# Gate and up projections by seven block products per tile pair, feed-forward in two chunks

## What is computed

```python
def half_ffn(x, g, w_gate, w_up, w_down):
    h = rmsnorm(x, g)
    return 0.5 * ((jax.nn.silu(h @ w_gate) * (h @ w_up)) @ w_down)
```

## Time and profile before

| what | value |
|---|---|
| median of three runs | 2231.39 us (2229.24 to 2231.44) |
| profiled execution | 2230.26 us |
| its span | 2228.7 us |
| PE, DVE, ACT, POOL busy | 98%, 48%, 35%, 3% |
| matmuls recorded | 18340 |
| weights and data read, written | 188.5 MB, 8.05 MB |
| mean rate of the transfers | 89 GB/s |

### The profile page before, as it was taken

One profiled execution on the slowest core, in us unless ns is written; L12 is line 12 of the kernel. 1 busy time (PEld: TensorE's weight loads), 2 busy tenths in 40 slices (PEclk: granted clock), 3 DMA queues, 4 the chain that ended last, 5 costly groups with the idle time before them and its releaser, 6 DMA issues.

```text
span 2228.7 us, 41911 instructions
## 1 busy us (share of the span) xinstructions
PE 2174.9 (98%) x18340; PEld 2115.3 (95%) x18340; DVE 1067.8 (48%) x1536; ACT 769.9 (35%) x1060; POOL 66.8 (3%) x140
## 2 busy tenths in 40 slices
PE   7999999999988999999999999999999999999998
PEld 7999999998887899999999999999997599999997
DVE  5444433586555544444334444433568545444332
ACT  5222222344244442222223222222357633222222
POOL 0000000100110000000000000000102300000000
PEclk9999999999998999999999999999999999999999
DMA  4333333433200323333333333333324323333231
GB/s 135 99 87 94 93 90 86 115 89 82 77 7 2 100 87 94 94 87 93 95 88 95 89 92 96 91 88 98 100 67 143 125 76 104 87 95 95 88 92 59
DMA packets 355286, 199.15 MB, mean 89 GB/s; under 512 B 10070, under 2 KB 350194, under 8 KB 355096
## 3 DMA queue, kind: packets, MB, share of 16 engines
q1 hardware_dynamic: 346768, 174.49, 27.3%
q0 software_dynamic: 6160, 19.84, 3.1%
q10 hardware_dynamic: 2176, 2.15, 0.3%
HBM read 188.52 MB, written 8.05 MB: 88 GB/s over the span
## 4 chain that ended last, share of the span: by engine, by line
PE 93%; DVE 4%; ACT 2%; issue 1%; DMA 0%; ACTq 0%; DVEq 0%
PE PS L2136 84%; PE PS L2244 4%; PE PS L2784 1%; PE PS L2703 1%; PE PS L2717 0%; PE PS L2686 0%; DVE X L1681 0%; PE PS L2151 0%; PE PS L2769 0%; PE PS L2706 0%; PE PS L2589 0%; PE PS L2312 0%; DVE wlo L1356 0%; DMA prow_f<-in_ln_ffn 0%; DVE skX L1960 0%
## 5 line engine op out<-in xcount | busy, mean ns | idle before, releaser
L2136 PE MATMUL PS<-hh,whi 128*128 128x260 f32 x3600 | 729.4, 284 | 3.1 <-DVE hl L2059 1.8
L2136 PE MATMUL PS<-hh,wlo 128*128 128x260 f32 x3600 | 726.0, 283 | 0.0
L2136 PE MATMUL PS<-hl,whi 128*128 128x260 f32 x3600 | 725.0, 283 | 0.0
L1356 DVE TENSOR_TENSOR wlo<-stage,whi 128x1024 fp32r<-128x1024 f32 x337 | 412.3, 1223 | 471.2 <-ACT whi L771 467.6
L2136 PEld LDWEIGHTS PS<-hh,whi 128*128 128x128 f32 x3600 | 556.4, 189 | 6.0 <-DVE small L1495 1.5
L2136 PEld LDWEIGHTS PS<-hh,wlo 128*128 128x128 f32 x3600 | 555.6, 189 | 0.0
L2136 PEld LDWEIGHTS PS<-hl,whi 128*128 128x128 f32 x3600 | 554.2, 188 | 0.0
L771 ACT ACTIVATE whi<-stage 128x1024 fp32r<-128x1024 f32 x337 | 352.9, 1049 | 282.4 <-PE PS L2136 270.6
L2136 PE MATMUL PS<-act_h,whi 128*128 128x260 f32 x1408 | 284.0, 283 | 0.0
L2136 PE MATMUL PS<-act_h,wlo 128*128 128x260 f32 x1408 | 283.2, 282 | 0.0
L2136 PE MATMUL PS<-act_l,whi 128*128 128x260 f32 x1408 | 282.5, 282 | 0.0
(11 more groups left out here) (427 smaller groups left out, 1554.1 us busy)
## 6 DMA issues: line engine op xcount, KB each, us to landing
stage<-in_ffn_w_gate SPq DMA_DIRECT2D x88, 512.0 KB, 3.8
stage<-in_ffn_w_up SPq DMA_DIRECT2D x88, 512.0 KB, 3.8
stage<-in_ffn_w_down SPq DMA_DIRECT2D x64, 512.0 KB, 3.7
stage<-in_w_in_e SPq DMA_DIRECT2D x28, 512.0 KB, 3.8
stage<-in_ffn_w_down SPq DMA_DIRECT2D x32, 384.0 KB, 3.4
stage<-in_w_in_o SPq DMA_DIRECT2D x20, 512.0 KB, 3.7
stage<-in_w_out_e SPq DMA_DIRECT2D x8, 512.0 KB, 3.7
stage<-in_w_out_o SPq DMA_DIRECT2D x8, 512.0 KB, 3.7
```

The source lines that it names most:

```text
L1356: dve.tensor_tensor(wlo[:, slot, :], stage[:, s % STAGE_SLOTS, :], whi[:, slot, :].bitcast(F32), ALU.subtract).then_inc(lo_ready, 1)
L2136: mm = pe.matmul(psum[:, half, :], w, x(k)[:, half * HALF:(half + 1) * HALF], start=first and w is hi and x is rhs_hi, stop=last and w is lo)
```

## The change

For the output tile pairs 2 to 10 of each feed-forward (MODES "S"), gate and up are each computed as one **group** of seven block products; pairs 0 and 1 (HEAD, "P") stay plain units. A group takes the two output tiles as block columns of the weights, even and odd contraction tiles as block rows, and the two token halves as block columns of the input, which makes a 2x2 by 2x2 block product; the scheme has seven products and sums around them. A product (`block_product`) is 4 contraction tiles x 3 = 12 matmuls of 260 columns into one PSUM bank, so a group has 84 matmuls where two units have 96.

- The weights of a group (1 MB) come in one transfer to half of a doubled staging place (`stage`, `stage_x`). ACT and DVE split them in four batches: a (1024 columns), b (512, into `w4h` and `w4l`), c and d (1024 each). Between these DVE forms four sums of 4x128 columns in place (`sum_of`), which batches c and d then split. The batches of the next group are made while this one's products run.
- The sums of the input blocks are formed once per feed-forward during the head: four operations of 260 columns per tile of `ht_h` and `ht_l`, a copy of `xb` by ACT, and a split of 1040 columns.
- Products go to four PSUM banks, in the order P1, P6, P2, P5, P3, P7, P4, and each bank is used again. ACT copies P1 to `snapT`; DVE adds the others in seven block sums (`add`): U2, C11, V, C12, U3, C22, C21. Then gate is multiplied by rstd, Silu is applied by ACT, and up multiplies it without rstd, which the down projection's update applies.
- The feed-forward goes in two CHUNKS: pairs 0 to 5, then the down projection of their 12 tiles, then pairs 6 to 10 and the down projection of 10 tiles; activations have 12 places instead of 22. A down output tile has two pieces per chunk (8 and 4, 6 and 4 contraction tiles), and its update is two DVE operations (`update_down`) in each chunk.
- The stage loops are written out, and a plan (`BATCHES`, `LOADS`) sets slots, places and counts of the waits ahead of time.

```diff
+CHUNKS = ((0, 6), (6, 11))
+MODES = ("PP", "PP") + ("SS",) * 9
+HEAD = 2
+DOWN_PAIRS = (2, 3, 1, 0, 2, 1, 0, 3)
+DOWN_ORDER = [(0, 0), (1, 0), (0, 1), (1, 1)] + [(m, p) for m in range(2, 8) for p in range(2)]
+ORDER = ("P1", "P6", "P2", "P5", "P3", "P7", "P4")
+PRODUCTS = {"P1": ("a", 0), "P2": ("a", 1), "P3": ("d", 1), "P4": ("b", 0), "P5": ("c", 0), "P6": ("c", 1), "P7": ("d", 0)}
...
+def ffn_events(chunks=CHUNKS, modes=MODES):
+    events, group = [], 0
+    for c, (t0, t1) in enumerate(chunks):
+        for t in range(t0, t1):
+            for up in range(2):
+                if modes[t][up] == "S":
+                    events.extend(("prod", group, which, t, up) for which in ORDER)
+                    group += 1
+            for n in (2 * t, 2 * t + 1):
+                events.extend(("unit", n, up) for up in range(2) if modes[t][up] == "P")
+        events.extend(("piece", c, m, p) for m, p in DOWN_ORDER)
+    return events

...
+            def make():
+                batch = BATCHES[made[0]]
+                act.wait_ge(w_loaded[batch.load.quarter], batch.load.count)
+                if batch.kind == "c":
+                    act.wait_ge(sums, 4 * batch.group + 3)
+                if batch.kind == "d":
+                    act.wait_ge(sums, 4 * batch.group + 4)
+                if batch.free:
+                    act.wait_ge(unit_done, batch.free)
+                act.activation(split_out(batch, False), staged(batch), ACT.Copy).then_inc(hi_ready, 1)
+                made[0] += 1
...
+                def group_step(g, which, t, up, done, late):
+                    own = BY_FIRST[f, g, "a"].n + (6 if MODES[t][1] == "P" else 4)
+                    q = GROUPS * f + g
+                    if which == "P1":
+                        if late:
+                            high(late.pop())
+                        reach(done)
+                        if q:
+                            act.wait_ge(block_sum, BLOCK_SUMS * (q - 1) + C11_SUM)
+                        act.activation(snapT[:, 2, :], PS[:, banks_of(q)["P1"], 0:HALF], ACT.Copy).then_inc(p1_copied, 1)
+                        ahead(done, own - 1)
+                    elif which == "P2":
+                        ahead(done, own)
+                    elif which == "P5":
+                        ahead(done, own + 1)
+                    elif which == "P3":
+                        ahead(done, own + 2)
+                        half_of(2 * t, up)
+                    elif which == "P7":
+                        ahead(done, own + 3)
+                    elif which == "P4" and up:
+                        late.append(2 * t + 1)
+                    elif which == "P4":
+                        silu(2 * t + 1)
...
+                if batch.kind in ("a", "b"):
+                    half = (stage if batch.load.quarter < 2 else stage_x)[:]
+                    k = half.rearrange("p s (k n) -> p (s k) n", n=2 * P)
+                    a11, a21 = k[:, 0::2, 0:P], k[:, 0::2, P:2 * P]
+                    a12, a22 = k[:, 1::2, 0:P], k[:, 1::2, P:2 * P]
+                    if batch.kind == "a":
+                        dve.wait_ge(lo_ready, batch.n + 1)
+                        sum_of(batch, 0, a11, a11, a21, ALU.subtract)
+                        sum_of(batch, 1, a21, a21, a22, ALU.add)
+                    else:
+                        dve.wait_ge(lo_ready, batch.n + 1)
+                        sum_of(batch, 2, a22, a22, a11, ALU.subtract)
+                        sum_of(batch, 3, a12, a12, a22, ALU.subtract)
...
+                        t1, t2, t3, t4 = (snapT[:, m, :] for m in range(4))
+                        b11, b12, b21, b22 = xb[:, 0:HALF], xb[:, HALF:TOK], x1[:, 0:HALF], x1[:, HALF:TOK]
+                        dve.wait_ge(t_act, X_TURNED + 2 * (KP * f + n) + 1)
+                        if count:
+                            dve.wait_ge(t_dve, count)
+                        dve.tensor_tensor(t1, b12, b11, ALU.subtract).then_inc(t_dve, 1)
+                        dve.scalar_tensor_tensor(out=t3, in0=b22, scalar=g1, in1=b12, op0=ALU.mult, op1=ALU.subtract)\
+                           .then_inc(t_dve, 1)
+                        dve.wait_ge(t_dve, count + 1)
+                        dve.scalar_tensor_tensor(out=t2, in0=b22, scalar=g1, in1=t1, op0=ALU.mult, op1=ALU.subtract)\
+                           .then_inc(t_dve, 1)
+                        dve.wait_ge(t_dve, count + 3)
+                        dve.scalar_tensor_tensor(out=t4, in0=b21, scalar=g1, in1=t2, op0=ALU.mult, op1=ALU.subtract)\
+                           .then_inc(t_dve, 1)
+                    else:
+                        product(n, pair(2 * (n % 2) + 1))
+                        dve.wait_ge(t_act, X_TURNED + 2 * (KP * f + n) + 2)
...
+                        dve.tensor_tensor(ht_l[:, :, n, :], snapT[:], ht_h[:, :, n, :].bitcast(F32), ALU.subtract)\
+                           .then_inc(t_dve, 1)
+                        low(n)
...
+                def half_of(n, up, q):
+                    dve.wait_ge(block_sum, BLOCK_SUMS * q + (C21_SUM if n % 2 else C12_SUM))
+                    if up:
+                        product(n, None)
+                    else:
+                        dve.tensor_tensor(tmp[:, n % 2, :], tmp[:, n % 2, :], rstd[:], ALU.mult).then_inc(gate_read, 1)
+                def add(q, number, out, in0, in1, of_own=0):
+                    if of_own:
+                        dve.wait_ge(block_sum, BLOCK_SUMS * q + of_own)
+                    dve.tensor_tensor(out, in0, in1, ALU.add).then_inc(block_sum, 1)
...
+                def group_step(g, which, t, up, done, late):
+                    q = GROUPS * f + g
+                    own = BY_FIRST[f, g, "a"].n + (6 if MODES[t][1] == "P" else 4)
+                    bank = {w: PS[:, n, 0:HALF] for w, n in banks_of(q).items()}
+                    u2, u3, p1 = (snapT[:, n, :] for n in range(3))
+                    (c11, c12), (c21, c22) = ([tmp[:, a + 2 * up, h * HALF:(h + 1) * HALF] for h in range(2)] for a in range(2))
+                    if which == "P1":
+                        if late:
+                            low(late.pop())
+                        ahead(done, own - 1)
+                    elif which == "P2":
+                        reach(done)
+                        if q:
+                            dve.wait_ge(block_sum, BLOCK_SUMS * q)
+                        dve.wait_ge(p1_copied, q + 1)
+                        add(q, U2_SUM, u2, p1, bank["P6"])
+                        if base + 2 * t >= 2:
+                            dve.wait_ge(act_lo if up else prod_ready, base + 2 * t - 1)
+                        add(q, C11_SUM, c11, p1, bank["P2"])
+                        ahead(done, own)
+                    elif which == "P5":
+                        ahead(done, own + 1)
+                    elif which == "P3":
+                        reach(done)
+                        add(q, V_SUM, c12, u2, bank["P5"], U2_SUM)
+                        add(q, C12_SUM, c12, c12, bank["P3"], V_SUM)
+                        half_of(2 * t, up, q)
+                        ahead(done, own + 2)
+                        if up:
+                            low(2 * t)
+                    elif which == "P7":
+                        reach(done)
+                        add(q, U3_SUM, u3, u2, bank["P7"])
+                        dve.wait_ge(act_lo if up else prod_ready, base + 2 * t)
+                        add(q, C22_SUM, c22, u3, bank["P5"], U3_SUM)
+                        ahead(done, own + 3)
+                    elif which == "P4":
+                        reach(done)
+                        add(q, C21_SUM, c21, u3, bank["P4"])
+                        half_of(2 * t + 1, up, q)
+                        if up:
+                            late.append(2 * t + 1)
...
+            def update_down(s, f, c, m, done):
+                reach(done)
+                psum, y, x = pair(DOWN_PAIRS[m]), two(tmp[:, 2 + m % 2, :]), two(xT[:, m, :])
+                dve.scalar_tensor_tensor(out=y, in0=psum, scalar=0.5, in1=two(rstd[:]), op0=ALU.mult, op1=ALU.mult)\
+                   .then_inc(x_part, 1)
+                dve.wait_ge(x_part, 3 * KD * f + (2 * KD + m if c else 2 * m) + 1)
+                dve.tensor_tensor(x, x, y, ALU.add).then_inc(x_ready if c else x_part, 1)
...
+            def block_product(batch, at, x_hi, x_lo, bank, alone):
+                hi, lo = (slot_w(batch.slot, low) for low in (False, True))
+                for j in range(KP):
+                    c = (j if alone else 2 * j + at) * P
+                    for n, (w, x) in enumerate(((hi, x_hi), (hi, x_lo), (lo, x_hi))):
+                        mm = pe.matmul(PS[:, bank, 0:HALF], w[:, c:c + P], x[:, j, :], start=j == 0 and n == 0,
+                                       stop=j == KP - 1 and n == 2)
+                mm.then_inc(unit_done, 1)
...
+                def group_product(g, which, t, up):
+                    q = GROUPS * f + g
```

(17 more changed lines are left out.)

675 lines of the change are left out of this document (424 added, 251 removed).

## The result

| what | before | after |
|---|---|---|
| median | 2231.41 us (2229.24 to 2233.72, 4 runs) | 2303.72 us (2302.43 to 2304.68, 4 runs) |
| span of the profiled execution | 2228.7 us | 2302.6 us |
| PE, DVE, ACT, POOL busy | 98%, 48%, 35%, 3% | 92%, 69%, 40%, 3% |
| matmuls recorded | 18340 | 17476 |

The change makes the kernel **slower by 3.2%**: ratio 1.0324, 95% interval 1.0306 to 1.0341. The forecast was 2294 us in a range of 2255 to 2365.

A forecast was written before the change was run, and what follows sets the result against it. PE, 98% busy, was taken as the bound before the change, DVE after it. 2230.3 us plus 61 (four feed-forwards at +15.3) plus 2.7 of small things gave 2294 us, range 2255 to 2365.

The forecast's parts named there:

- PE's saving: Gate and up groups: 864 fewer matmuls at 0.1201 us, 103.8 us of PE, 20.2 us per pair instead of 23.07.
- DVE ends last, 24.4 us of work per pair: Gate and up groups: DVE's summed operations take 24.4 us per pair against PE's 20.2, so DVE sets the time.
- Gate group 12.05, up group 13.27, pair 25.3: DVE's path through the two groups, operations spaced with overlap plus waits for ACT: 25.3 us per pair, 2.26 more than before.
- The new wait for ACT's copy: After a gate group, the next U2 waits for ACT's copy of P1, queued behind the silu: 0.99 us.
- the 0.71 for ACT's high half: In the up group, DVE waits 0.71 us for the high half of the activation from ACT.
- Edges of the blocks: Per feed-forward: head 46.1 us, hand-over wait 2.2, start to first U2 4.5, last U2 to PE's leaving 5.2.
- The first feed-forward's +2: Head of the first feed-forward: DVE starts late and has more to do, some 2 us.
- elsewhere the next stage's first unit covers it: Residual updates at stage ends: the added second operation costs 0.7 us once, at the last update; elsewhere it is hidden.
- One feed-forward +15.3: Each whole feed-forward takes 395.8 us against 380.5 now, 15.3 more; four times, +61 us.
- Clock: PE's granted clock stays at 1.00 in the groups despite short idle times; its fall was a rival given 22%.
- The rival's price: Clock rival: at 1.2 GHz P6 and P2 take 5.2 us, not 2.9; +68 us, kernel 2362; chance 22%.
- DVE's share, "75% or so": Whole kernel: DVE's busy share was to rise from 48% to 75% or so.

The follow-up runs named there:

- with gate alone: Changed kernel with only the gate projections of pairs 2 to 10 by seven block products, up by plain units: 2203.57 us, ratio to before 0.9876.
- the kernel with mended edges: Seven products for gate only; PE waits for turned sums at P6; exactly two next-stage splits between the last two tiles' updates: 2181.73 us, ratio to before 0.9787.
- two doses: Changed kernel with weight sums made on one column per block of 128: all four sums of a group, 2174.2 us; one of four, 2272.1 us.

## Why the prediction was right, and where it was off

Right in sign, and 10 us (0.4%) low; that it is so near is in part luck, since a missed term and an oversized one worked against each other.

- *PE's saving* was forecast as 864 matmuls, 20.2 us per pair if PE ended last. The matmuls are gone, and their price holds: with gate alone 432 matmuls are saved, 51.9 us at 0.1201; the kernel with mended edges is 2229.6 - 2181.7 = 47.9 us faster than the kernel before beside it, the one with the changed kernel's edges only 27.9.
- *DVE ends last, 24.4 us of work per pair.* This is the step on which all rested, and it held: 22.89 us busy per pair against 23 forecast, and the period follows DVE's work one to one in two doses. The prices held as well: 0.42 for 260 columns (forecast 0.425), 0.69 for 512, 1.22 for the split, with the overlap of 0.085 us between operations that don't wait for each other. Two sums at 105.35 and 105.68 are 0.33 apart for an operation of 0.42, and the pair has room for no more: the 0.115 per hand-over that the prediction worked out from the page "VectorE: DVE Perf Modes" of the Trainium skill, section "The DRAIN you can't avoid", does not appear.
- *Gate group 12.05, up group 13.27, pair 25.3.* U2 to U2 is 12.20 and 13.25, the pair 25.45; the P1 copies, forecast to alternate with 12.05 and 13.3, stand 12.45 and 13.00 apart. The 0.15 more lies in small spacings, such as 0.52 from 126.32 to 126.84 where 0.455 was taken, and 0.51 from 117.89 to 118.40 where 0.34 was.
- *The new wait for ACT's copy* was forecast as 0.99 of the path and shows as 1.08 of waiting; *the 0.71 for ACT's high half* as 0.71. What the forecast didn't say is how little it is worth to remove the first: 0.26 per pair.
- *Edges of the blocks.* The way from the last U2 to PE's leaving was forecast as 5.2; it is 967.05 to 972.03 in the second feed-forward, 4.98. The way from the hand-over to the first U2 was forecast as 4.5. In the third and fourth feed-forward it is 4.63 and 4.61 (1273.24 to 1277.87, 1936.33 to 1940.94), as forecast. In the second it is 872.34 to 878.49, 6.15, and in the first 6.93, since there the clock falls behind PE's idle time. **That was a missed term**, at two of four hand-overs: the forecast had the wait (2.2, measured 1.94 at three of them), but not the clock behind it, although it weighed just this for the groups.
- *The first feed-forward's +2* came out as +3.7 over the second: 2.4 us more of waiting at the hand-over, 0.8 more to the first U2, and 0.4 more at the transition (2.37 us against 1.93).
- **The step that failed**, though the forecast as a whole held, is *"elsewhere the next stage's first unit covers it"*. The forecast looked at the second operation of each update and found 0.7 us with a cover. It didn't look at what stands between the last updates in DVE's and ACT's order: splits of weights whose transfer is late. With two pieces of 6 and 4 tiles in place of one of 22, an output tile gives only 7.2 us where it gave 15.84, and that time no longer holds a late transfer, three splits and two updates. This costs 1.9 to 2.4 us and a fall of the clock in three places.
- *One feed-forward +15.3.* The last, which has a hand-over and no transition, has +13.6, so groups and block edges were sized 1.7 us too high each time. The place is the first gate group of the second block: DVE has made the first of the next group's splits and two of its sums while it had nothing else to do, waits 2.02 and 1.36 us for PE, and the group takes 10.06 us (U2 at 2108.05 and 2118.11) where the walk took 12.05. Four times 13.6 is 54.4 in place of 61; the transitions add 5.2 and 4.8 in the second and third feed-forward, transition and late head 8.9 in the first, and the rest 0.6: 73.9 in place of 63.7. The oversized term hid a part of the missed one. Of the 5.2 in the second, 1.5 is the clock at its hand-over.
- *Clock.* "Stays at 1.00" is right in the groups, where PE idles 1.29 and 1.10 us with work between (123.98 and 126.79), and wrong at the edges. The rival's price was not refuted: where the clock did fall in groups of 84 matmuls, with the sums on GpSimd, P6 and P2 took 4.7 us to DVE's U2 where the forecast has 2.9 and 0.3, and DVE waited 2.04 us for them. It was the rival's condition that did not come.
- *DVE's share, "75% or so".* An error of arithmetic: the forecast's own terms, 1067.8 us and 36 times 13.9, make 68% of 2294, and 69% was measured.

## What to carry to other kernels

A scheme that trades matmuls for element-wise work is worth what is left of the slower engine's period: add up both engines' work per tile, and apply the scheme to as many tiles as keep the two near each other. Here it paid for half of the projections (-1.2%, and -2.1% with the stage ends reordered) and cost where it was used for all (+3.2%).

Work ahead for the next stage belongs between two urgent steps only as far as its data is there. Three splits there, the third of them with a late transfer, cost 13 us against two (some 2.4 of them, by the traces, the clock at the first hand-over); none cost 22 us. A transition that was covered by a long tile must be costed again when tiles get shorter.

A neighbour's idle engine is not free capacity when the moved work sits in a chain: ask which wait the moved step feeds.

## What the runs showed of the hardware that was not expected

- With sums running on GpSimd (1.44 to 1.46 us each), VectorE's 520-column operation with both inputs in SBUF took 1143 ns on average (L1737, 72 of them) against 700 without, and single ones 1.78 us; the one of 260 columns with an input in PSUM stayed at 0.43. What GpSimd's sums take with VectorE idle no run shows.
- In the changed kernel PE's clock fell from 2.4 to 1.2 GHz in or just behind five single idle times of 1.9 us and more (72.95, 428.72, 872.34, 1227.53, 1627.06), and not behind two of 1.94 us (1273.24, 1936.33). It stayed at 2.4 GHz through dozens of pairs with idle times of 0.5 to 1.4 us between products. With a third of each group's matmuls gone and waits up to 2.8 us it fell within the groups too, and so it did with the sums on GpSimd, where PE's waits for DVE's sums go up to 3.8 us.
- The same idle time at the same place can go either way: 2.86 or 2.87 us, 12 matmuls after the head's last, let the clock fall in four kernels and left it at 2.4 GHz in two. The length of an idle time alone does not decide, and what does stays open.

Not tried: sums on GpSimd for one of the four alone, or seven products for up in some pairs only.
